# Mixer gates and output products in row form: tokens stationary, 512 weight columns moving

## The reference, cut to what matters

```
proj = u @ w_in                                    # 1024 x 14336
xa, ya, q, k, v, g, sb, sc, sh, gates = split(proj)
oa = (rg_lru(conv(xa)) * gelu(ya)) @ w_lru_out     # 1024 x 1024
ret = retention(q, k, v)                           # 4 heads, each 256 x 512, each row scaled by its rms
ob = (silu(g) * ret) @ w_ret_out                   # 2048 x 1024
oc = (sb * conv(sc * sh)) @ w_sc_out               # 1024 x 1024
ga, gb, gc = split(sigmoid(gates))                 # three times 1024 wide
return (ga * oa + gb * ob + gc * oc) @ w_mix_out   # 1024 x 1024
```

## Time and profile before

| | |
|---|---|
| median of 3 runs | 2057.03 us (2056.74 to 2057.04) |
| the profiled execution: its own time | 2055.96 us |
| the profiled execution: span | 2054.2 us |
| TensorE busy with matmuls | 2023.5 us, 99% of the span, 13404 matmuls |
| VectorE busy | 1318.7 us, 64% |
| ScalarE busy | 969.8 us, 47% |
| mean granted TensorE clock | 0.999 of full |
| moved by DMA | 369.54 MB, 180 GB/s |

### The profile page before, as it was taken

One profiled execution on the slowest core, in us unless ns is written; L12 is line 12 of the kernel. 1 busy time (PEld: TensorE's weight loads), 2 busy tenths in 40 slices (PEclk: granted clock), 3 DMA queues, 4 the chain that ended last, 5 costly groups with the idle time before them and its releaser, 6 DMA issues.

```text
span 2054.2 us, 31600 instructions
## 1 busy us (share of the span) xinstructions
PE 2023.5 (99%) x13404; PEld 1848.5 (90%) x13404; DVE 1318.7 (64%) x1617; ACT 969.8 (47%) x1334; POOL 102.6 (5%) x211
## 2 busy tenths in 40 slices
PE   9999999999999999999999999999999999999997
PEld 8888998999999888888889999999988889989986
DVE  7656778457556664766569755565667556666565
ACT  5445465344434543544454643343444445654443
POOL 1003000000000000100200000000010101010000
PEclk9999999999999999999999999999999999999999
DMA  7556355534556455555564464455655655354552
GB/s 253 198 187 212 126 189 198 185 124 165 196 179 209 155 196 194 173 196 198 186 200 159 153 218 147 146 185 185 205 181 170 229 199 171 126 166 172 184 200 81
DMA packets 282027, 369.54 MB, mean 180 GB/s; under 512 B 6679, under 2 KB 253751, under 8 KB 281886
## 3 DMA queue, kind: packets, MB, share of 16 engines
q1 hardware_dynamic: 276864, 352.34, 51.2%
q0 software_dynamic: 4528, 14.85, 2.3%
q10 hardware_dynamic: 494, 0.32, 0.1%
HBM read 366.28 MB, written 1.08 MB: 179 GB/s over the span
## 4 chain that ended last, share of the span: by engine, by line
PE 94%; DVE 4%; ACT 2%; issue 1%; POOL 0%; DMA 0%; DVEq 0%; POOLq 0%; ACTq 0%
PE ps L1505 22%; PE ps L1488 15%; PE ps L1476 13%; PE ps L1478 13%; PE ps L1477 13%; PE ps L1489 7%; PE ps L1558 4%; DVE w_lo L978 1%; PE ps L1532 1%; DVE u L1035 1%; PE ps L1632 1%; DVE a L1136 1%; ACT u L672 1%; PE ps L1817 1%; PE ps L1540 0%
## 5 line engine op out<-in xcount | busy, mean ns | idle before, releaser
L978 DVE TENSOR_TENSOR w_lo<-raw,w_hi 128x1024 fp32r<-128x1024 f32 (+1 forms) x658 | 766.6, 1207 | 326.6 <-ACT w_hi L638 325.7
L638 ACT ACTIVATE w_hi<-raw 128x1024 fp32r<-128x1024 f32 (+1 forms) x658 | 652.8, 1041 | 393.7 <-PE ps L1505 205.2
L1476 PE MATMUL ps<-u,w_hi 128*128 128x256 f32 x1712 | 491.5, 287 | 1.6 <-DVE w_lo L978 1.5
L1478 PE MATMUL ps<-u,w_lo 128*128 128x256 f32 x1712 | 484.4, 283 | 0.0
L1477 PE MATMUL ps<-u,w_hi 128*128 128x256 f32 x1712 | 484.3, 283 | 0.0
L1488 PE MATMUL ps<-u,w_hi 128*128 128x512 f32 x1280 | 451.1, 397 | 0.0
L1489 PE MATMUL ps<-u,w_lo 128*128 128x256 f32 x1280 | 359.2, 281 | 0.0
L1476 PEld LDWEIGHTS ps<-u,w_hi 128*128 128x128 f32 x1712 | 328.4, 192 | 5.1 <-issue 4.6
L1477 PEld LDWEIGHTS ps<-u,w_hi 128*128 128x128 f32 x1712 | 328.4, 192 | 2.4 <-issue 1.9
L1478 PEld LDWEIGHTS ps<-u,w_lo 128*128 128x128 f32 x1712 | 328.4, 192 | 0.0
L1488 PEld LDWEIGHTS ps<-u,w_hi 128*128 128x128 f32 x1280 | 240.3, 188 | 58.6 <-issue 0.8
(11 more groups left out here) (263 smaller groups left out, 2278.4 us busy)
## 6 DMA issues: line engine op xcount, KB each, us to landing
raw<-in_w_mix_in_dram SPq DMA_DIRECT2D x112, 1024.0 KB, 5.0
raw<-in_ffn_w_in_dram SPq DMA_DIRECT2D x88, 1024.0 KB, 5.0
raw<-in_ffn_w_out_dram SPq DMA_DIRECT2D x40, 1024.0 KB, 4.8
raw<-in_w_ret_out_dram SPq DMA_DIRECT2D x16, 1024.0 KB, 5.1
raw<-in_w_up_dram SPq DMA_DIRECT2D x16, 1024.0 KB, 5.4
raw<-in_w_down_dram SPq DMA_DIRECT2D x16, 1024.0 KB, 4.9
raw<-in_w_in_dram SPq DMA_DIRECT2D x9, 1024.0 KB, 5.7
raw<-in_w_lru_out_dram SPq DMA_DIRECT2D x8, 1024.0 KB, 5.2
```

Source lines behind the costliest of these rows:

```text
L638: A(parts(n)[0][:, part], raw[i % RAW][:, part], ACT.Copy).then_inc(heads_done, 1)
L978: V.tensor_tensor(parts(n)[1][:, part], raw[i % RAW][:, part], parts(n)[0][:, part], ALU.subtract)\
L1476: M(dst[a], hi[:, k, c], act_hi[:, k0 + k, :], start=first and k == 0, stop=False)
L1478: ins = M(dst[a], lo[:, k, c], act_hi[:, k0 + k, :], start=False, stop=last and k == KD - 1)
```

## The change

Seven stages (`ga`, `lru_out`, `g`, `gb`, `ret_out`, `gc`, `sc_out`: 4+4+8+4+8+4+4 = 36 slots a layer, 72 in all) change to a second row form, `half_slot`: a slot is 512 weight rows of 512 columns; 24 matmuls with 512 moving columns go to a pair of banks, one bank for each 128 tokens (banks 2, 3 for even column halves, 0, 1 for odd ones). Two slots (four in `ret_out`) complete a half. Gates, `a5` and the head's silu(g) are now held with tokens on partitions; ScalarE and VectorE take a pair of banks after its last slot. The scaled head is multiplied with silu(g) straight from banks 5 and 6 into `mul2`, then turned into banks 7 and 4 one slot later than before, copied to `h_hi` by ScalarE, and `h_lo` is taken by VectorE. The mixed sum is turned by 8 transposes for each half (`turn_mixed`), copied to `u_hi` by ScalarE (`mix_heads`) and `u_lo` is taken by VectorE.

```diff
+ROW_FORM = {"ga": 2, "lru_out": 2, "g": 2, "gb": 2, "ret_out": 4, "gc": 2, "sc_out": 2}
+        def half_bank(e, tt):
+            return ps[:, (2 + 2 * e) % 4 + tt, :]
+        def ret_bank(i):
+            return ps[:, 4 if i else 7, :]
...
 # ScalarE, in mixer(l), the turn of slot n
+            def mix_heads(l, e):
+                for tt in range(TT):
+                    act.wait_ge(mix_turned.sem, mix_turned.at(l, 2 * e + tt + 1))
+                    A(u_hi[:, 4 * e:4 * e + 4, P * tt:P * tt + P], half_bank(e, tt).rearrange("p (k n) -> p k n", n=P),
+                      ACT.Copy).then_inc(mix_head.sem, 1)
...
                         ahead(n)
-                        if name in ("xa", "ya", "ga", "g", "sc", "gb", "gc"):
+                        if name in ("xa", "ya", "sc") or name in ("ga", "g", "gb", "gc") and j % 2 == 1:
                             emptied(n)
...
+                        elif name == "g" and j % 2 == 1:
+                            h = j // 2
+                            if h >= 2:
+                                act.wait_ge(ret_scaled.sem, ret_scaled.at(l, h - 1))
+                            for tt in range(TT):
+                                A(columns_of(a2, h % 2, tt), half_bank(h % 2, tt), ACT.Silu).then_inc(g_ready.sem, 1)
...
+                        if name == "mix_out" and j == 0:
+                            mix_heads(l, 0)
+                        elif name == "mix_out" and j == 1:
+                            mix_heads(l, 1)
+                        if name in ("g", "sc") and (m - 35) % 2 == 0 and 0 <= (m - 35) // 2 < HEADS:
+                            h = (m - 35) // 2
+                            act.wait_ge(ret_turned.sem, ret_turned.at(l, h + 1))
+                            for i in range(2):
+                                A(h_hi[:, 4 * h + 2 * i:4 * h + 2 * i + 2, :], ret_bank(i).rearrange("p (k n) -> p k n", n=S),
+                                  ACT.Copy).then_inc(ret_head.sem, 1)
...
 # VectorE, in mixer(l); (m - 34) % 2 == 0:
-                            dve.wait_ge(ret_turned.sem, ret_turned.at(l, h + 1))
+                            dve.wait_ge(ret_scale.sem, ret_scale.at(l, h + 1))
                             dve.wait_ge(g_ready.sem, g_ready.at(l, 2 * h + 2))
...
+                            for tt in range(TT):
+                                ins = V.scalar_tensor_tensor(mul2[:, tt, :], ps[:, 5 + tt, :], ret_rs[:, tt:tt + 1],
+                                                             columns_of(a2, h % 2, tt), ALU.mult, ALU.mult)
+                            ins.then_inc(ret_scaled.sem, 1)
+                        if name in ("g", "sc") and (m - 35) % 2 == 0 and 0 <= (m - 35) // 2 < HEADS:
+                            h = (m - 35) // 2
+                            for i in range(2):
+                                dve.wait_ge(ret_head.sem, ret_head.at(l, 2 * h + i + 1))
+                                ks = slice(4 * h + 2 * i, 4 * h + 2 * i + 2)
+                                ins = V.tensor_tensor(h_lo[:, ks, :], ret_bank(i).rearrange("p (k n) -> p k n", n=S),
+                                                      h_hi[:, ks, :], ALU.subtract)
+                            ins.then_inc(ret_ready.sem, 1)
                         ahead(n)
...
+                        elif name == "sc_out" and j % 2 == 1:
+                            e = j // 2
                             dve.wait_ge(slot_used, n + 1)
+                            dve.wait_ge(gc_ready.sem, gc_ready.at(l, 2 * e + 2))
+                            for tt in range(TT):
+                                acc = columns_of(a5, e, tt)
+                                own.done(V.tensor_tensor(mul2[:, tt, :], half_bank(e, tt), columns_of(a4, e, tt), ALU.mult))
+                                V.tensor_tensor(acc, acc, mul2[:, tt, :], ALU.add).then_inc(mixed.sem, 1)
+                        if name == "mix_out" and j < 2:
+                            for tt in range(TT):
+                                dve.wait_ge(mix_head.sem, mix_head.at(l, 2 * j + tt + 1))
...
+                                V.tensor_tensor(u_lo[:, ks, tok], half_bank(j, tt)..., u_hi[:, ks, tok], ALU.subtract)
+                                 .then_inc(mix_ready.sem, 1)
...
 # TensorE; scores(l, h):
+                if h >= 2:
+                    pe.wait_ge(ret_ready.sem, ret_ready.at(l, h - 1))
 # attend(l, h):
-                    pe.wait_ge(ret_ready.sem, ret_ready.at(l, h))
+                    pe.wait_ge(ret_scaled.sem, ret_scaled.at(l, h))
 # turn_head(l, h), after slot 34 + 2h:
                 pe.wait_ge(ret_scaled.sem, ret_scaled.at(l, h + 1))
+                if h < HEADS - 1:
+                    pe.wait_ge(ret_probs.sem, ret_probs.at(l, h + 2))
...
+            def half_slot(n, k0, act_hi, act_lo, e, first, last):
+                hi, lo = half_view(n)
+                for i in range(4):
+                    if i % 2 == 0:
+                        split_part(n, i // 2)
+                    for tt in range(TT):
+                        tok = slice(P * tt, P * tt + P)
+                        for a, (stat, mov) in enumerate(((act_hi, hi), (act_hi, lo), (act_lo, hi))):
+                            ins = M(half_bank(e, tt), stat[:, k0 + i, tok], mov[:, i, :], start=first and i == 0 and a == 0,
+                                    stop=last and i == 3 and a == 2)
+                ins.then_inc(slot_used, 1)
...
                             if j < 2:
-                                pe.wait_ge(mix_ready.sem, mix_ready.at(l, j + 1))
+                                pe.wait_ge(mix_ready.sem, mix_ready.at(l, 2))
...
                                 row_slot(n, (2 * j, 2 * j + 1), u_hi, u_lo, j == 0, False)
+                                if j == 0:
+                                    turn_mixed(l, 1)
...
+                            row_form(l, name, j)
+                            if name == "sc_out" and j == 2:
+                                turn_mixed(l, 0)
```

More of the change, by code:

```diff
@@ L329, in build @@
         ret_turned = signal("ret_turned", HEADS)
+        ret_head = signal("ret_head", 2 * HEADS)
         ret_ready = signal("ret_ready", HEADS, 1)
@@ L336, in build @@
         gc_ready = signal("gc_ready", 4)
+        mixed = signal("mixed", 4)
+        mix_turned = signal("mix_turned", 4)
+        mix_head = signal("mix_head", 4)
         mix_ready = signal("mix_ready", 4)
@@ L1167, in mixer @@
                             h = (m - 34) // 2
-                            dve.wait_ge(ret_turned.sem, ret_turned.at(l, h + 1))
+                            dve.wait_ge(ret_scale.sem, ret_scale.at(l, h + 1))
                             dve.wait_ge(g_ready.sem, g_ready.at(l, 2 * h + 2))
[L1171 to L1180, removed]
+                            if h >= 1:
+                                dve.wait_ge(ret_turned.sem, ret_turned.at(l, h))
+                            for tt in range(TT):
[10 more added lines that the diff above has]
+                            ins.then_inc(ret_ready.sem, 1)
                         ahead(n)
@@ new lines, in turn_mixed, with row_form @@
+            def turn_mixed(l, e):
+                for tt in range(TT):
+                    pe.wait_ge(mixed.sem, mixed.at(l, 2 * e + tt + 1))
+                    for i in range(4):
+                        ins = nc.tensor.transpose(half_bank(e, tt)[:, P * i:P * i + P],
+                                                  columns_of(a5, e, tt)[:, P * i:P * i + P], ident[:, :])
+                    ins.then_inc(mix_turned.sem, 1)
+            def row_form(l, name, j):
+                n = l * SLOTS + AT[name] + j
+                per = ROW_FORM[name]
+                e = j // per % 2
+                if j % per == 0:
+                    if name == "g" and j >= 4:
+                        pe.wait_ge(g_ready.sem, g_ready.at(l, j - 2))
+                    else:
+                        before = EMPTIED[BEFORE[name]]
+                        pe.wait_ge(before.sem, before.at(l, 2 * e + 2))
+                if name == "lru_out" and j == 0:
+                    pe.wait_ge(oa_ready.sem, oa_ready.at(l, 4))
+                if name == "ret_out" and j == 0:
+                    pe.wait_ge(ret_ready.sem, ret_ready.at(l, HEADS))
+                if name == "sc_out" and j == 0:
+                    pe.wait_ge(oc_ready.sem, oc_ready.at(l, 4))
+                ah, al = (h_hi, h_lo) if name in ("lru_out", "ret_out", "sc_out") else (u_hi, u_lo)
+                half_slot(n, 4 * (j % per), ah, al, e, j % per == 0, j % per == per - 1)
@@ L1737, in mixer @@
-                        if name == "g" and j % 2 == 1:
-                            turn_head(l, j // 2)
+                                last_rows(n, 4, u_hi, u_lo, rows_done.sem,
+                                          ready=[(mix_ready.sem, mix_ready.at(l, 3 + tt)) for tt in range(TT)])
+                        elif name in ROW_FORM:
+                            row_form(l, name, j)
```

(13 more changed lines are left out.)

118 lines of the change are left out of this document (41 added, 77 removed).

## The result

The changed kernel takes 2076.66 us (median of 4 runs, 2075.89 to 2076.98) against 2056.99 us (4 runs of the kernel before): +19.7 us, a ratio of 1.0094 with a 95% interval of 1.0082 to 1.0106. It is slower, over the 2061 us that the prediction set for that, inside the range of 2064 to 2080 and 4.7 us above the 2072 forecast.

What follows compares the result with a forecast made beforehand. TensorE's issue pace was taken as the bound. Terms -22.5 + 0.6 + 3.5 + 15.4 + 13.2 + 5.2 = +15.4 us on the profiled 2055.96 gave 2071.4, called 2072 for the median; range 2064 to 2080.

Steps and rivals of the forecast that it cites:

- scores(2) and scores(3): In g, PE newly waits 3.27 us before each for the preceding head's copies and lows: 6.5 us a layer.
- before slot 72: At the start of mix_out, PE newly waits 6.6 us for u_lo of the mixed sum's first half: +13.2 us in all.
- turn_head(3): After slot 40 in g, PE newly waits for the scaled head 3: +1.15 us a layer.
- shape, turned sum and ga together: 72 slots with fewer, wider matmuls -22.5 us, extra transposes of the mixed sum +3.5, longer wait in ga +0.6: -18.4.
- the clock at mix_out: PE idles 6.4 us before slot 72, so its clock falls in both layers: 2 x 2.6 = +5.2 us.
- the clock in g: Gaps of 3.1 us in g are under 4.9 us, so no clock fall was counted there: 0 us.
- Rival B: Three row-form matmuls in a row into one bank cost 7 ns in every matmul: +12.1 us, 2084 us; chance 4%.
- Rival E: The new matmul shape saves little, 4.3 us instead of 22.5: 2090 us; chance 2%.
- Rival D: Scores(2), scores(3) and slot 72 find their signals given, as the chains aren't behind the slots' ends: 2038.6 us; chance 4%.
- Rival A: The clock falls in g too, at four gaps of 3.1 us: 10.4 us more, 2083 us; chance 7%.
- Rival C: The clock never falls, not even in the gaps before slot 72: 2067 us; chance 15%.

Runs made afterwards that it cites:

- both reorderings: Changed kernel with head copies and lows moved before the slot's end and the mixed sum's first half before slot 71's end: 2039.68 us, 0.9909 of before.
- The first two experiments: Changed kernel with head copies and lows before the slot's end: 2055.9 us; changed kernel with the mixed sum's first half before slot 71's end: 2059.4 us.
- the run with overlong fills: Changed kernel with idle matmuls before scores(2), scores(3) and slot 72, twice as long as meant: 2087.43 us, 1.0142 of before.
- the second graded kernel: Changed kernel with 10, 6, 3 and 0 idle matmuls before the four scores waits in g, in order of time: 2075.02 us (one run).

## Why the prediction was right

Its direction and the places of its new waits were right; the waits at scores(2) and scores(3) were right to 0.03 us each, that before slot 72 to 0.13, that at turn_head(3) to 0.16. The clock's term was wrong: it left out the falls in g. By its own steps, for the whole kernel:

| step | predicted | measured |
|---|---|---|
| shape, turned sum and ga together | -18.4 | -18.2 (both reorderings against before, 2 x 9.1) |
| scores(2) and scores(3) | +13.1 | 4 x 3.24 = +13.0 |
| turn_head(3) | +2.3 | 2 x 0.99 = +2.0 |
| before slot 72 | +13.2 | 2 x 6.47 = +12.9 |
| the clock at mix_out | +5.2 | 2 x 2.1 = +4.2 |
| the clock in g | 0 | 4 x 1.7 = +6.8 |
| start of the kernel | 0 | -1.2 |
| sum | +15.4 | +19.5 |

*Shape.* The row pace was carried over from v1 and held. Rival B (one bank costs) fell with the alternating banks, and no bank cost shows. Rival E is out too: 36 slots gave 11 us a mixer and not 2.2. The Trainium skill's 2.5 ns above N/2.4, on which it stood (TensorE: Matmul & The Clock Gate, "Back-to-back issue gap"), is given there for an isolated matmul; the stream here, with a weight load for each matmul, stands 13.5 ns above.

*The waits.* Their sizes came from adding up starts on record in a boundary, which has the same pair of instructions, and from reading each engine's program in order. Rival D said that ACT might get to the copies in time, having idle time enough. It had (1.80 us idle just before), and so had DVE, with 11.84; neither helped, since what they did next was fixed. The first two experiments together make D true by moving the same instructions, and its 2038.6 is then 2039.7 on one chip and 2038.6 on another.

*The failed step* is "Gaps of 3.1 us in g are under 4.9: none counted". The 4.9 us came from one fall, after the last matmul of the kernel, and was taken for a threshold. It was one sample of a delay, and the longest of its kind: at the same place the clock fell 2.4 to 4.9 us after the last matmul in the twelve executions that were profiled, 3.5 us after it in the changed kernel's (2063.5, 2067.0). At the waits inside the mixers it fell 2.4 to 5.3 us after PE had stopped, and it fell even where PE had gone on meanwhile. The two windows of PE before and after the fall in the run with overlong fills, whose last matmul ended at 2075.3:

```profile
2075.30:2077.66 2.36, 0.00 (x0) 1.00 0.52 197
2077.68:2079.00 1.32, 0.00 (x0) 0.50 0.12 42
```

The term that stood at nothing measured +6.8. Rival A had the mechanism, at 7%, and too high a price, 4 x 2.6 = 10.4: behind the waits in g the lower level lasted 3.4 us and not 5.2, so 1.7 each. The idle matmuls and the copies moved ahead show that it is the gap and not thin work. Rival C (the clock never falls) is out: it fell at mix_out in all eight gaps that the four kernels with an unfilled one show.

*What the result owes to chance.* That the total lies in the range is in part luck. The 2080 allowed for falls at mix_out that cost double, and they cost less than forecast; what filled that room were the falls in g, which the prediction had as rival A and put outside, at 2083. The start's -1.2 us hides part of the clock's term too; it depends on when the clock comes up in an execution (11.1 and 8.8 us in these two, 9.2 to 12.6 in the ten others), and on nothing in the change. So does the price of a fall at mix_out: PE worked at half pace for 3.5 to 5.7 us behind the same wait of 6.47 us in four kernels, 1.8 to 2.9 us lost, and the 4.2 for both in the table is what this execution drew.

## What to carry to other kernels

When an operation is moved to another engine, place it in that engine's program by what it needs, and look at what stands ahead of it: here two copies and two subtractions, ready to run for a whole slot, stood behind a wait for the end of that slot, and made a reshaping worth 18 us cost 20. On TensorE, where it is otherwise never idle, price each new wait of some 2.5 us or more twice, for the wait and for the lowered clock behind it (1.4 to 2.9 us a fall here; waits of 1.8 us and less lowered nothing); if the wait can't be moved, idle matmuls in it give the second part back, provided they end before it does.

## What the runs showed of the hardware

- TensorE's clock fell after waits that made PE 2.5 us late (twice of two), 3.24 us (nine times of ten) and 6.5 us (eight of eight), not after 1.8 or 0.9 (twice of two each). The fall came 2.4 to 5.3 us after PE had stopped, and can come when PE is at work again (up to 1.4 us after, in the second graded kernel), so the slow stretch is to be looked for behind the gap too.
- The lower level lasted 3.4 us behind each of the eleven waits of 2.5 and 3.24 us that lowered it, and 6.8 us at each of the eight of 6.5 us; how much of that falls on PE's work differs from execution to execution.
- Halving the number of matmuls at equal work gave 13 ns for each one saved (0.120 for 256 columns, 0.227 for 512), in float32r with a weight load for each.
- Three 512-column matmuls in a row into one PSUM bank run at the pace of alternating ones (21.76 and 21.79 us for 96).
